# A decoder layer with 32 experts: each expert's token gather reads one fp32 tile instead of three bf16 parts

## The reference

```python
def moe_ffn(u, w_router, b_router, w1, b1, w2, b2):
    logits = (u @ w_router + b_router).astype(jnp.float32)
    top_vals, top_idx = lax.top_k(logits, TOP_K)
    top_w = jax.nn.softmax(top_vals, axis=-1).astype(u.dtype)
    ...
    def body(acc, inp):
        tok, wt, e = inp
        hb = swiglu_clamped(u[tok] @ w1[e] + b1[e])
        yb = (hb @ w2[e] + b2[e]) * wt[:, None]
        return acc.at[tok].add(yb), None
```

## Time and profile before

| | value |
|---|---|
| median of three runs | 1405.76 us |
| lowest, highest | 1400.63, 1406.92 us |
| the profiled execution, its own time | 1401.74 us |
| its span in the profile | 1399.9 us |
| TensorE busy | 1307.5 us (93%) |
| VectorE busy | 390.9 us (28%) |
| ScalarE busy | 277.9 us (20%) |
| mean DMA rate over the span | 335 GB/s |
| mean DMA rate between 500 and 1350 us | 424 to 429 GB/s |

### The profile page before, as it was taken

How to read it: one execution, slowest core, us unless ns; L and a number is a source line. 1 busy time by engine, 2 the same in 40 slices (tenths; PEclk the granted TensorE clock), 3 DMA queues, 4 the chain that set the end, 5 groups by cost and what they waited for, 6 DMA issues and landing times.

```text
span 1399.9 us, 18601 instructions
## 1 busy us (share of the span) xinstructions
PE 1307.5 (93%) x7435; PEld 667.2 (48%) x7435; DVE 390.9 (28%) x942; ACT 277.9 (20%) x633; POOL 43.2 (3%) x48
## 2 busy tenths in 40 slices
PE   9999998999999999998989989999889999888996
PEld 5687787655886543343333333333333343333332
DVE  1055456677212531121111211112211221122112
ACT  3124325475100311111111111111111111111111
POOL 3000100020000000000000000000000000000000
PEclk9999999999999999999999999999999999999999
DMA  8733334353966599999999999999999999999995
GB/s 270 216 122 111 131 121 136 106 140 103 309 248 237 198 427 430 428 428 428 427 429 429 428 428 427 429 429 428 428 428 414 432 428 428 428 430 428 428 428 242
DMA packets 73871, 468.49 MB, mean 335 GB/s; under 512 B 4867, under 2 KB 37915, under 8 KB 49228
## 3 DMA queue, kind: packets, MB, share of 16 engines
q1 hardware_dynamic: 70444, 457.89, 80.7%
q0 software_dynamic: 1952, 5.61, 1.4%
q10 hardware_dynamic: 1440, 4.52, 0.9%
HBM read 466.61 MB, written 1.13 MB: 334 GB/s over the span
## 4 chain that ended last, share of the span: by engine, by line
PE 55%; DMA 38%; ACT 2%; DVE 2%; issue 1%; SPq 1%; POOL 0%; DVEq 0%; ACTq 0%; POOLq 0%
PE bank L1282 53%; DMA ring<-in_w 26%; DMA arena<-in_w 12%; DMA arena<-in_c_oh 1%; SPq L419 1%; PE bank L1394 0%; PE bank L1685 0%; ACT wdt L822 0%; ACT arena L737 0%; ACT arena L651 0%; PE bank L1324 0%; PE bank L1576 0%; DVE ring L981 0%; ACT arena L831 0%; DVE arena L1115 0%
## 5 line engine op out<-in xcount | busy, mean ns | idle before, releaser
L1282 PE MATMUL bank<-ring,arena 128*64 128x512 f32 (+3 forms) x2296 | 568.0, 603 | 55.2 <-DMA ring<-in_w 47.5
L1282 PEld LDWEIGHTS bank<-ring,arena 128*64 128x64 f32 (+2 forms) x2296 | 196.9, 144 | 384.1 <-issue 328.3
L1282 PE MATMUL bank<-arena 128*128 128x64 bf16 (+6 forms) x3052 | 358.1, 355 | 16.2 <-DMA arena<-in_w 13.1
L1282 PEld LDWEIGHTS bank<-arena 128*128 128x128 bf16 (+3 forms) x3052 | 173.4, 121 | 221.9 <-issue 190.0
L1282 PE MATMUL bank<-arena,ring 128*128 128x256 f32 (+2 forms) x1312 | 269.8, 385 | 2.5 <-ACT decays L643 1.6
L1282 PEld LDWEIGHTS bank<-arena,ring 128*128 128x128 f32 (+1 forms) x1312 | 217.2, 181 | 45.3 <-ACT decays L643 1.8
L1196 DVE TENSOR_SCALAR arena<-bank 128x256 f32<-128x256 f32 x64 | 27.1, 423 | 687.2 <-PE bank L1282 687.2
L827 ACT ACTIVATE arena<-arena 128x256 f32<-128x256 f32 x64 | 26.7, 417 | 418.5 <-DVE arena L1196 418.5
L834 ACT ACTIVATE arena<-bank 128x512 f32<-128x512 f32 x32 | 19.1, 597 | 276.8 <-PE bank L1282 276.8
L1282 PE MATMUL bank<-arena,wdt 64*128 64x512 f32 (+1 forms) x280 | 70.5, 603 | 1.7 <-issue 1.0
L827 ACT ACT_TABLE_LOAD x32 | 41.1, 1283 | 0.6
(11 more groups left out here) (236 smaller groups left out, 594.5 us busy)
## 6 DMA issues: line engine op xcount, KB each, us to landing
ring<-in_w SPq DMA_DIRECT2D x128, 2048.0 KB, 25.3
arena<-in_w SPq DMA_DIRECT2D x64, 2048.0 KB, 29.2
ring<-in_w_in SPq DMA_DIRECT2D x34, 1024.0 KB, 6.2
ring<-in_w_ssm SPq DMA_DIRECT2D x8, 1024.0 KB, 7.7
arena<-cum_rows ACTq DMA_DIRECT2D x8, 512.0 KB, 5.3
ring<-in_w_att SPq DMA_DIRECT2D x16, 256.0 KB, 6.8
ring<-in_w_out SPq DMA_DIRECT2D x4, 1024.0 KB, 4.8
arena<-bias_rows POOLq DMA_DIRECT2D x1, 2048.0 KB, 11.4
```

What stands on the lines that cost most here:

```text
L1282: return tn.matmul(o, lhsT, rhs, start=first, stop=last, skip_group_check=True)
```

## The change

The bf16 parts are gone. Every gather now does what `gather_first` did: 16 fp32 matmuls on `acc` and `gsel0`. `split_u` is removed from DVE's work ahead of the first expert. Since `acc` has to stay as it is, `glu` and `sig`, two scratch tiles that lay over it, move to the place where the parts were. `slots_of` writes the fp32 matrix `gsel0` in place of the bf16 `gsel`. What each engine waits for is unchanged.

```diff
-        upart = at(R + 10240, 3, 2, D, dt=BF16)
...
-        glu, sig = at(4736, 2, 256), at(4224, 2, 256)
+        glu, sig = at(R + 10240, 2, 256), at(R + 10752, 2, 256)
...
-        gsel = at(SM, 2, CAP, dt=BF16)
...
             def slots_of(col):
                 for c in range(2):
-                    ins = v.tensor_scalar(gsel[:, c, :], iota2[:, 0:CAP], pos[:, c, bass.ds(col, 1)], None, ALU.is_equal)
+                    ins = v.tensor_scalar(gsel0[:, c, :], iota2[:, 0:CAP], pos[:, c, bass.ds(col, 1)], None, ALU.is_equal)
                 ins.then_inc(g_ready, 1)
...
-            def split_u(c):
-
-                ch.link(v.tensor_copy(upart[:, 0, c, :], acc[:, c, :]))
-                for part in range(1, 3):
-                    ch.link(v.tensor_tensor(acc[:, c, :], acc[:, c, :], upart[:, part - 1, c, :], ALU.subtract))
-                    ch.link(v.tensor_copy(upart[:, part, c, :], acc[:, c, :]))
...
-                    for c in range(2):
-                        split_u(c)
...
                 pe.wait_ge(g_ready, n + 1)
                 for k in range(KT):
-                    for part in range(3):
-                        for c in range(2):
-                            ins = mm(bank[7][:, CAP * k:CAP * k + CAP], upart[:, part, c, P * k:P * k + P],
-                                     gsel[:, c, :], part == 0 and c == 0, part == 2 and c == 1)
+                    for c in range(2):
+                        ins = mm(bank[7][:, CAP * k:CAP * k + CAP], acc[:, c, P * k:P * k + P], gsel0[:, c, :], c == 0, c == 1)
                 ins.then_inc(gat_ready, 1)
```

## The result

The changed kernel takes 1408.11 us in the median of 16 runs (1406.22 to 1411.95), the kernel before 1405.42 us in 16 runs beside it. The ratio is 1.0036, 95% interval 1.0024 to 1.0047: **slower by 0.36%, 5 us**. It is a loss, within the 0.5% that I had set as the line. The profiled execution took 1407.39 us, its span is 1405.5 us.

A forecast was written before the change was run, and what follows sets the result against it. The weight stream at 429 GB/s was taken as the bound, TensorE having 3.35 us per expert to spare. Start 1.05, turn 2.0 and tail 2.0 sum to +5.05 us: 1406.7 or 1410.8, predicted 1409 us, range 1402 to 1417.

The forecast's parts named there:

- The gather: Each expert's gather on TensorE: 16 fp32 matmuls for 48 bf16 ones make it 2.0 us longer.
- cheap gather: Rival: in the loop columns or passes, not loads, set the gather's pace; +0.6 or +0.9 us in sum; chance 0.09.
- Place 1: Start of the weight stream: the issue waiting for expert 0's w2 comes later, stream idle 1.05 us.
- Place 2: Turn of the issue order at expert 20: the queue is already dry, so all 2.0 us count.
- Place 3: After the last w1 part lands: the last gather is on the path, 2.0 us.
- The sum: Start, turn and tail of the kernel together: 5.05 us slower.
- Meeting the stream: TensorE uses up its prefetch lead and waits for landings again: after 12 experts, and after the turn by expert 30.
- cliff: Rival, loop after expert 20: from +2.4 us per gather TensorE never catches up; +17 us at +3.0; chance 0.14.
- DVE: Ahead of the first expert: removing ten split operations, 9.4 us of DVE, gains nothing, as w1 of expert 0 covers them.
- 1409 us: Predicted time of the whole kernel, between 1406.7 (from the profiled execution) and 1410.8 (from the median).

The follow-up runs named there:

- half-column kernel: Changed kernel with its fp32 gathers moving 32 instead of 64 columns, leaving out every expert's upper 32 slots; one run, 1429.64 us.
- small dose: Kernel before with the bf16 gather's first block computed four times in all experts, 0.57 us more per gather; ratio to before 1.0011.
- even kernel: Kernel before with the bf16 gather's first block computed 13 times in experts 0, 2, 4 and so on, 2.25 us more; ratio to before 1.0028.
- split kept: Changed kernel with VectorE's ten split operations put back ahead of the first expert, into scratch tiles; ratio to the kernel before 1.0036.
- bf16 gather ahead of part 2: Kernel before with its bf16 gather called ahead of w1 part 2 of each expert instead of behind part 3; ratio to before 1.0006.

## Why the prediction was right

- **The gather, +2.0.** 2.2 measured. The first gather's pairs took 110 ns, those in the loop 116. That the loads set the pace is shown by the half-column kernel; the cheap gather (columns or passes) falls.
- **Place 1, the start, 1.05 us.** This is the term that was mis-sized: TensorE paid 2.3 us at A, and the landing it waits for came 2.5 us later. The idle time of the stream, which is what I had worked out, is only a part of the error. Before, then after, from 24 to 40 us behind the start of the first gather:

```profile
502.96:518.96 16.00, 16.00 (x80) 5.66 (x78) 0.00 (x0) 1.88 (x2) 0.00 (x0) 1.00 1.01 430
502.02:518.02 16.00, 15.55 (x80) 5.88 (x80) 0.60 (x2) 2.81 (x5) 0.00 (x0) 1.00 0.95 388
```

388 instead of 430 GB/s over 16 us is 1.6 us of transfer, where the sum gives 1.25 with the gather as measured. So the queue did still have data for part of the delay; in the small dose the same stretch has 427 GB/s, a loss of 0.1 of its 0.57 us. What the forecast left out is that the landings moved further than the data. Before, the transfer issued at 505.90 landed 4.9 us behind the one ahead, the stream's own step. After, it was issued 2.2 us later (from the first gather on) and landed 2.5 us later, 7.4 behind the one ahead. In ten profiles in which this issue comes 29.0 to 30.0 us after the first gather's start it took 7.7 to 10.1 us to land, against 7.7 for the one issued at 487.27 with nothing else moving. What sets this time is open.
- **Place 2, the turn, 2.0.** 2.3 (B less A), the gather's 2.2. Counted as transfer the dent grew by more, as these stretches show (before, then after, 592 to 608 us behind the first gather's start):

```profile
1070.96:1086.96 16.00, 15.54 (x78) 5.67 (x78) 0.61 (x2) 2.82 (x5) 0.00 (x0) 1.00 0.97 398
1070.02:1086.02 16.00, 15.54 (x86) 7.44 (x87) 2.25 (x8) 2.81 (x5) 0.00 (x0) 1.00 0.79 316
```

That is 3.1 us, and with the 1.6 of the start 4.7, which is B's 4.6. The lateness of the landings that was not idle time at the start became idle time here, where the queue ran empty.
- **Place 3, the tail, 2.0.** 2.2, and 0.0 in the even kernel.
- **The sum.** +5.05 against +6.6 in the profiles from the first gather on, so 1.5 us short, 1.3 of them in place 1. That the timed ratio says +5 is in part luck. The executions of both kernels fall into two groups, and the shares differ: before, 6 of 16 lie about 1400.8 us and 9 about 1406.2, after, 9 lie about 1406.9 and 6 about 1411.9. Group against group the loss is 6.1 and 5.6 us.
- **Meeting the stream.** Expert 13, one later than the sum's 12; after the turn I said by expert 30, it was 31, so nearly not at all. The measured gather, +2.2, is 0.2 us short of the +2.4 from which the cliff begins, and that is how close the kernel is to it.
- **DVE, nothing.** Shown twice, by the split kept, and by the bf16 gather ahead of part 2 for the price without the cover.
- **1409 us.** I had put it between the two groups of times of the same kernel, and the median came out between them too, at 1408.11. That it is so near is luck, as it hangs on how many executions fall into each group.

## What to carry to other kernels

When a stream bounds a loop, as here, work added to the other engine costs only where the stream starts, where it runs dry and after its last landing: name these places, and test them by lengthening the same step in even and in odd iterations. Then count the room per iteration and the iterations left to catch up, because beyond it each microsecond counts in every one. Fewer instructions are no gain by themselves: 16 fp32 matmuls took 2.5 times as long as 48 bf16 ones, since their stationary loads set the pace (3.65 of the 3.72 us).

## What the runs showed of the hardware that was not expected

With 32 columns in the gather the granted TensorE clock fell although TensorE never waited for a transfer. The chain of the half-column kernel in order of time:

```profile
509.19 28.48 PE bank L1271 x140
...
539.02 26.88 PE bank L1271 x140
...
567.21 28.47 PE bank L1271 x140
```

A stretch of it (after TensorE's work stand granted clock, DMA share and GB/s):

```profile
600.00:800.00 200.00, 196.82 (x1014) 86.98 (x1012) 35.18 (x98) 25.53 (x49) 0.00 (x0) 0.97 1.01 428
```

and one of the changed kernel:

```profile
500.00:1070.00 570.00, 554.39 (x2902) 250.74 (x2900) 100.03 (x279) 72.98 (x140) 0.00 (x0) 1.00 1.01 427
```

The same 140 instructions take 1.6 us longer in every other expert, and the mean granted clock is 0.97 where it is 1.00 with 64 columns: it goes down to the lower of its two levels, 1.2 GHz, for part of those pieces (0.58 on average from 534 to 536 us). What TensorE did just before is the gather of 3.7 us (530.40 to 534.09), busy with loads and hardly with columns; but behind the next expert's gather, 560.23 to 563.91, the clock stays at 1.00. The slow pieces put the period at 29.0 us on average. That leaves 0.35 us of room per expert, where the forecast's cliff begins below 0.95, and the kernel pays as at the cliff. That the narrow gather is what lowers the clock fits these rows, but it is one profile, no run tried it apart, and why only every other expert is hit is open.
